# Moving one block of experts from place 7 to place 15 in the order of a mixture-of-experts stage

## The chip, the cores and the metric

The kernel runs on one core of one Trainium2 chip. The metric is the device time of one launch in microseconds (us). A profiled execution of the kernel before gave the trace that is read here. In the text PE is TensorE (matmul), DVE VectorE, ACT ScalarE, POOL GpSimd and SP SyncE; "L511" is line 511 of the kernel.

## The reference

One decoder block on 1024 tokens of width 1024, in float32: adaLN, a projection, gated linear attention and differential attention, a merge, and then a mixture of experts. Only the last part matters here:

```python
p_g = softmax(xf @ w_rg + b_rg);  p_top, g_idx = top_k(p_g, 1)
pe_top, e_loc = top_k(softmax(e_logits[group g_idx]), 2)       # two of the 8 experts of one group
weights = p_top * pe_top / sum(pe_top)
yb = (silu(xb @ w1[e]) * (xb @ w3[e])) @ w2[e]                 # w1, w3: 1024 x 512, w2: 512 x 1024
out[token] += yb * weight;      x = x + gate2 * out
```

There are 32 experts. Each has three matrices of 2 MB, so that all of them are 201 MB.

## The kernel before

The first 960 us or so are the attention part and the router. The expert stage follows and runs to the end.

**Blocks.** The experts are ranked by how many tokens chose them. A rank gets 2 to 4 groups of 32 rows (`PARTS`), and four groups make a block of 128 rows: 22 blocks in all. `TURN` (L51) is the order in which the blocks are worked, and `QUADS[n]` the four ranks of the block at place n. Some blocks hold one rank alone, as (4,4,4,4). Others hold two, as (26,26,27,27).

**Passes.** A block has three passes on PE. Pass 0 multiplies its rows by w1, pass 1 by w3 and pass 2 by w2. Each is 32 matmuls of a 32-column stationary tile against 512 columns (64 records in the trace, as float32 goes twice). From place 3 on, PE's order is: transposes of the hidden rows of block n-1 (L1431), passes 0 and 1 of block n, transposes of the rows of block n+1 (L1348), pass 2 of block n-1. This order stands in `PASSES` (L53).

**Weight buffers.** Ten buffers of 2 MB each hold one matrix. When a pass meets a matrix that isn't loaded yet, the planner (L63 to L69) gives it the buffer whose last use comes first, and `FREED_BY` notes the pass that frees it. SP walks the matrices in the order of their first use (L574 to L582). For each it waits until PE has done the freeing pass and then starts the load (L511). Ahead of its first matmul a pass waits for its matrices (L1410, L1441). The first 12 and the last 14 of these loads are cut in two halves (`HALVED`, L515 and L520), the 60 between them are whole. I number these 60 as F1 to F60. A block brings three loads for each rank in it that is new.

**POOL.** For each block POOL gathers the token rows (L722) and adds the results to the output by an indirect DMA with accumulation (L737). A block with two ranks has two such scatters, one behind the other.

Each matrix is loaded once. A rank whose groups lie in two blocks that stand far apart keeps its three buffers in between: rank 13 does so from place 4 to place 14, so that seven buffers turn over in that stretch.

The change reaches what depends on `TURN`: `QUADS`, `PASSES`, the planner's `BUF` and `FREED_BY`, the list of loads, the segments of the scatters and the column of the tables that a block reads.

Of the kernel before, what the change touches and what calls it, by code (L numbers as in the profile page):

```python
# [47 lines left out]
GROUPS = [r for r in range(NE) for _ in range(PARTS[r])]  # L48
NB = len(GROUPS) * G // P
assert NB * P == len(GROUPS) * G and NB % 2 == 0  # L50
TURN = (1, 0, 2, 16, 10, 17, 3, 19, 4, 7, 8, 9, 5, 18, 11, 12, 14, 13, 15, 20, 6, 21)  # L51
QUADS = [GROUPS[4 * v:4 * v + 4] for v in TURN]
PASSES = [(w, b) for b in range(3) for w in range(2)] + [(2, 0), (2, 1)] + [x for b in range(3, NB) for x in ((0, b), (1, b), (2, b - 1))] + [(2, NB - 1)]  # L53
NBUF = 10
# [15 lines left out]
LOADS = _n  # L70
assert len(set(QUADS[NB - 1])) == 2 and NB % 2 == 0 and TURN[NB - 1] >= NFB
LATE = list(FREED_BY)
# [49 lines left out]
def build(nc, io, out):  # L122

    with ExitStack() as ctx:
# [19 lines left out]
        def bank(b, n=1):  # L144
            return PS[:, b:b + n, :].rearrange("p b n -> p (b n)")
# [464 lines left out]
        def _(e):  # L610
# [107 lines left out]
            def gather(n, u):  # L718
                rows_done = NA * P if n == 0 else T
                if n >= 2:  # L720
                    e.wait_ge(s["m_tr"], 2 * n)
                e.indirect_dma_start(xg[u], None, xn_rows[0:rows_done],  # L722
                                     bass.IndirectOffsetOnAxis(tab_tok[:, TURN[n]:TURN[n] + 1], 0),
                                     bounds_check=rows_done - 1, oob_is_err=False).then_inc(xg_ld[u], 16)

            def scatter(n, u):
                e.wait_ge(s["m_y"], n + 2 if n < NB - 1 else n + 3)
                for i, (p0, p1) in enumerate(SEGS[n]):
                    if SEG_END[n] - len(SEGS[n]) + i > 0:
                        e.wait_ge(s["sc_done"], 16 * (SEG_END[n] - len(SEGS[n]) + i))  # L730
                    v = TURN[n]
                    idx = tab_tok[0:p1, v:v + 1] if p0 == 0 else seg_tok[0:p1 - p0, p0 // G - 1, v:v + 1]
# [1166 lines left out]
        def _(e):  # L1899
# [5 lines left out]
            def tsc(o, a, c1, op0, c2=None, op1=None):  # L1905
                if op1 is None:
                    return v.tensor_scalar(o, a, c1, None, op0)  # L1907
                return v.tensor_scalar(o, a, c1, c2, op0, op1)

            def stt(o, a, c, b, op0, op1):  # L1910
                return v.scalar_tensor_tensor(out=o, in0=a, scalar=c, in1=b, op0=op0, op1=op1)  # L1911
# [755 lines left out]
            def weighted(n, u):  # L2667
                e.wait_ge(s["m2_mm"], 2 * n + 3)
                if n >= 2:
                    e.wait_ge(s["sc_done"], 16 * SEG_END[n - 2])  # L2670
                stt(yb[u], bank(6, 2), tab_w[:, TURN[n]:TURN[n] + 1], gate[:, 1, :], ALU.mult, ALU.mult).then_inc(s["m_y"], 1)

# [16 lines left out]
            def same_rows():  # L2689
                e.wait_ge(s["mg_mm"], 1)  # L2690
                tsc(same, bank(5)[:, 0:P], tab_gap[:, TURN[NB - 1]:TURN[NB - 1] + 1], ALU.is_equal).then_inc(s["mg_in"], 1)
                e.wait_ge(s["mg_in"], 2)
# [59 lines left out]
```

## Time and profile before

| | us |
|---|---|
| median of 3 runs | 1499.81 (1498.01 to 1502.18) |
| the profiled execution's own time | 1502.34 |
| its span in the trace | 1500.6 |
| PE busy in the span | 1451.3 (97%) |
| PE's matmuls of all kinds | 8338 records |
| load queue of SP (q1) | 274.51 MB |
| POOL's DMA queue (q0) | 16.77 MB |

The span is the time from the first to the last instruction in the trace; the execution takes 1.7 us more. PE is busy nearly all the time, and the DMA engines are busy nearly all of the last third. The stage has to be read for both.

### The profile page before, as it was taken

Reading aid. Unit: us, or ns where it says so; the run is one execution under the profiler, and the core shown is the slowest. Engines: PE = TensorE matmul, PEld = TensorE weight load, DVE = VectorE, ACT = ScalarE, POOL = GpSimd, SP = SyncE. Lnnn points to the kernel's source line nnn. Section 1 sums busy time; section 2 is a strip of 40 time slices with the busy share of each in tenths; the row PEclk is TensorE's granted clock in tenths of the full one; section 3 lists DMA queues with packets and bytes.
Section 4 is the critical chain, followed back from the end, with each engine's and each line's share of the span. In section 5 each row is a group of like instructions: output and inputs, shape, how many; then the busy total and the mean of one; then the engine's idle time right before and its main releaser. Section 6 shows DMA issues by size and latency. Waiting matters only on the chain. (4 is left out here: it accounts for less than half of the span.)

```text
span 1500.6 us, 20824 instructions
## 1 busy us (share of the span) xinstructions
PE 1451.3 (97%) x8338; PEld 706.0 (47%) x8338; DVE 580.6 (39%) x1186; ACT 339.9 (23%) x674; POOL 109.4 (7%) x142
## 2 busy tenths in 40 slices
PE   7999999999999999999999999999998899999996
PEld 3444456887876555444444444543332233333332
DVE  4497444646474237322222455661111011111111
ACT  3513332333236333111111122311110011111110
POOL 2000000000000000000000001001111111111111
PEclk9999999999999999999999999999999999999999
DMA  9790100000012110211121842599999999999994
GB/s 355 256 354 1 64 1 1 29 29 29 29 57 57 29 28 1 56 42 42 42 98 49 327 155 111 210 349 403 417 406 418 401 366 378 405 416 405 405 413 163
DMA packets 80280, 292.48 MB, mean 195 GB/s; under 512 B 13408, under 2 KB 42302, under 8 KB 61505
## 3 DMA queue, kind: packets, MB, share of 16 engines
q1 hardware_dynamic: 73634, 274.51, 46.6%
q0 software_dynamic: 6560, 16.77, 4.4%
q8 instruction: 61, 1.00, 0.3%
q14 instruction: 25, 0.20, 0.0%
HBM read 277.47 MB, written 20.09 MB: 198 GB/s over the span
## 5 line engine op out<-in xcount | busy, mean ns | idle before, releaser
L779 PE MATMUL PS<-R 128*32 128x512 f32 (+6 forms) x3965 | 785.1, 566 | 22.7 <-DMA R<-in_ada_w 9.4
L779 PEld LDWEIGHTS PS<-R 128*32 128x32 f32 (+3 forms) x3965 | 291.4, 132 | 400.2 <-issue 372.2
L779 PE MATMUL PS<-HT,R 128*32 128x512 f32 (+2 forms) x1424 | 340.3, 599 | 3.8 <-DMA HT<-in_expert_w 2.2
L1903 DVE TENSOR_TENSOR R<-R,PS 128x512 f32<-128x512 f32 x131 | 95.6, 746 | 472.8 <-PE PS L779 472.8
L779 PE MATMUL PS<-R,HT 128*128 128x512 f32 (+1 forms) x672 | 235.4, 506 | 3.1 <-ACT R L1526 1.5
L779 PEld LDWEIGHTS PS<-HT,R 128*32 128x32 f32 (+1 forms) x1424 | 113.4, 128 | 149.0 <-issue 148.1
L779 PEld LDWEIGHTS PS<-R,HT 128*128 128x128 f32 x672 | 125.7, 191 | 94.2 <-issue 81.4
L1526 ACT ACTIVATE R<-PS 128x512 f32<-128x512 f32 (+4 forms) x119 | 71.3, 610 | 430.8 <-PE PS L779 295.6
L779 PE MATMUL PS<-WK,R 128*32 128x512 f32 (+1 forms) x464 | 107.9, 601 | 0.0
L1911 DVE SCALAR_TENSOR_TENSOR R<-PS,R,gate 128x1024 f32<-128x1024 f32 (+1 forms) x23 | 28.5, 1238 | 129.8 <-PE PS L779 123.3
L737 POOL DMA_INDIRECT out_rows<-R x36 | 52.3, 1453 | 303.0 <-DVE R L1911 160.6
L1526 ACT ACTIVATE R<-PS,att_nm 128x128 f32<-128x128 f32 (+7 forms) x64 | 46.8, 736 | 108.8 <-DVE att_nm L1907 108.8
L1526 ACT ACTIVATE R<-PS,S,A 128x128 f32<-128x128 f32 x92 | 34.4, 456 | 159.0 <-PE PS L1348 159.0
L1903 DVE TENSOR_TENSOR R<-R 128x512 f32<-128x512 f32 (+13 forms) x95 | 59.2, 638 | 19.1 <-PE PS L779 16.3
L1526 ACT ACT_TABLE_LOAD x30 | 38.5, 1283 | 96.1 <-PE PS L779 93.6
L1526 ACT ACTIVATE R<-R 128x512 f32<-128x512 f32 (+7 forms) x49 | 31.8, 655 | 104.3 <-DVE R L1903 100.3
L1526 ACT ACTIVATE WK<-R 128x128 f32<-128x128 f32 (+2 forms) x56 | 34.2, 611 | 80.5 <-DVE R L1903 77.4
L2122 DVE TENSOR_REDUCE att_mx<-PS 128x2 f32<-128x256 f32 (+7 forms) x32 | 43.3, 1354 | 20.6 <-PE PS L779 20.4
L1526 ACT ACTIVATE WK<-PS 128x512 f32<-128x512 f32 (+9 forms) x50 | 30.6, 611 | 87.3 <-PE PS L935 48.7
L1911 DVE SCALAR_TENSOR_TENSOR R<-R,cact 128x2048 f32<-128x2048 f32 (+1 forms) x23 | 46.6, 2026 | 3.0 <-DMA R<-in_ada_w 0.6
L779 PE MATMUL PS<-R,gate 128*128 128x256 f32 (+1 forms) x224 | 47.1, 366 | 0.0
L779 PE MATMUL PS<-R,WK 128*128 128x128 f32 (+1 forms) x352 | 44.6, 279 | 2.1 <-DVE R L1907 1.6
(263 smaller groups left out, 851.8 us busy)
## 6 DMA issues: line engine op xcount, KB each, us to landing
R<-in_expert_w SPq DMA_DIRECT2D x36, 2048.0 KB
R<-in_expert_w SPq DMA_DIRECT2D x46, 1024.0 KB, 15.6
HT<-in_expert_w SPq DMA_DIRECT2D x17, 2048.0 KB, 21.8
HT<-in_expert_w SPq DMA_DIRECT2D x18, 1024.0 KB, 12.5
R<-in_ada_w SPq DMA_DIRECT2D x16, 1024.0 KB, 7.0
WK<-in_expert_w SPq DMA_DIRECT2D x7, 2048.0 KB
R<-in_w_in SPq DMA_DIRECT2D x24, 512.0 KB, 3.9
R<-in_ada_w SPq DMA_DIRECT2D x16, 512.0 KB, 10.7
```

Of the source, the lines that this page charges most:

```text
L737: e.indirect_dma_start(out, bass.IndirectOffsetOnAxis(idx, 0), rows_out, None, compute_op=ALU.add, bounds_check=T - 1, oob_is_err=False).t ...
L779: return nc.tensor.matmul(o, l, r, start=a, stop=z)
L1526: return nc.scalar.activation(o, i, f, **kw)
L1903: return v.tensor_tensor(o, a, b, op)
L1911: return v.scalar_tensor_tensor(out=o, in0=a, scalar=c, in1=b, op0=op0, op1=op1)
L2122: att(v.tensor_reduce(att_mx[:, i % 2, :], score_v[:, :, 0:(i + 1) * P], AX.X, ALU.max))
```

## The change

The block of ranks 26 and 27 (block number 19) leaves place 7 and goes to place 15. The blocks of places 8 to 15 each move up by one place.

```diff
-TURN = (1, 0, 2, 16, 10, 17, 3, 19, 4, 7, 8, 9, 5, 18, 11, 12, 14, 13, 15, 20, 6, 21)
+TURN = (1, 0, 2, 16, 10, 17, 3, 4, 7, 8, 9, 5, 18, 11, 12, 19, 14, 13, 15, 20, 6, 21)
```

The ranks by place, with the number of new matrices that the block brings:

| place | 6 | 7 | 8 | 9 | 10 | 11 | 12 | 13 | 14 | 15 | 16 | 17 | 18 |
|---|---|---|---|---|---|---|---|---|---|---|---|---|---|
| before | 4 | 26,27 | 5 | 8,9 | 9,10 | 10,11 | 6 | 24,25 | 13,14 | 14,15 | 17,18 | 16 + 17 | 18,19 |
| new | 3 | 6 | 3 | 6 | 3 | 3 | 3 | 6 | 3 | 3 | 6 | 3 | 3 |
| after | 4 | 5 | 8,9 | 9,10 | 10,11 | 6 | 24,25 | 13,14 | 14,15 | 26,27 | 17,18 | 16 + 17 | 18,19 |
| new | 3 | 3 | 6 | 3 | 3 | 3 | 6 | 3 | 3 | 6 | 6 | 3 | 3 |

(Block 17 works rank 16 and a last group of rank 17.) Rank 13 now holds its buffers up to place 13. Places 0 to 6 and 16 to 21 hold the same blocks as before. The number of loads, their sizes and which of them are cut in two stay as they are. The sequence of loads is the same up to F10. From F11 on the matrices of ranks 26 and 27 stand later in it, and many matrices lie in another buffer with another freeing pass.

## Rows read from the trace of the kernel before

**Rows 1.** The page: span, DMA's busy tenths and GB/s in 40 slices.

```profile
span 1500.6 us, 20824 instructions
...
DMA  9790100000012110211121842599999999999994
GB/s 355 256 354 1 64 1 1 29 29 29 29 57 57 29 28 1 56 42 42 42 98 49 327 155 111 210 349 403 417 406 418 401 366 378 405 416 405 405 413 163
```

**Rows 2.** Stretches: length, busy us by engine, PE's clock, DMA share, GB/s.

```profile
1100.00:1200.00 100.00, 87.95 (x752) 29.34 (x748) 11.86 (x19) 9.28 (x20) 13.24 (x10) 0.95 1.01 409
1200.00:1260.00 60.00, 60.00 (x548) 19.77 (x544) 10.59 (x18) 7.49 (x17) 8.96 (x7) 1.00 0.97 366
1260.00:1400.00 140.00, 140.00 (x1280) 45.36 (x1276) 21.19 (x36) 16.77 (x37) 22.06 (x17) 1.00 1.01 407
1131.00:1135.50 4.50, 4.50 (x28) 1.47 (x31) 0.00 (x0) 0.00 (x0) 0.00 (x0) 0.62 1.02 391
1193.30:1197.50 4.20, 4.20 (x24) 1.38 (x28) 0.00 (x0) 0.00 (x0) 1.42 (x1) 0.59 1.02 437
```

**Rows 3.** PE by time: start, us, line, names, count, [idle before].

```profile
1119.28 7.07 PE L779 MATMUL PS<-R 128*32 128x512 f32 x64 [1.33 <-DMA R<-in_expert_w]
1126.28 0.66 PE L1431 MATMUL PS<-ident,R 128*128 128x128 f32 x4
1130.92 0.62 PE L779 MATMUL PS<-R 128*32 128x512 f32 x2 [3.98 <-DMA WK<-in_expert_w]
...
1141.90 8.77 PE L779 MATMUL PS<-HT,R 128*32 128x512 f32 x64 [2.21 <-DMA HT<-in_expert_w]
...
1159.22 13.94 PE L779 MATMUL PS<-R 128*32 128x512 f32 x128
...
1181.70 7.07 PE L779 MATMUL PS<-HT,R 128*32 128x512 f32 x64
1193.30 8.77 PE L779 MATMUL PS<-R 128*32 128x512 f32 x64 [4.53 <-DMA R<-in_expert_w]
```

**Rows 4.** Four loads at L511: ns, start us, us to landing.

```profile
L511 SPq DMA_DIRECT2D HT<-in_expert_w x1: 332/332/332, 1110.3 to 1110.3; - x1
...
DMA to landing us min/median/max: 31.5/31.5/31.5
...
L511 SPq DMA_DIRECT2D HT<-in_expert_w x1: 332/332/332, 1217.9 to 1217.9; - x1
...
DMA to landing us min/median/max: 15.5/15.5/15.5
...
L511 SPq DMA_DIRECT2D HT<-in_expert_w x1: 336/336/336, 1322.7 to 1322.7; - x1
...
DMA to landing us min/median/max: 21.5/21.5/21.5
...
L511 SPq DMA_DIRECT2D HT<-in_expert_w x1: 333/333/333, 1382.2 to 1382.2; - x1
...
DMA to landing us min/median/max: 24.2/24.2/24.2
```

**Rows 5.** SP by time, columns as in rows 3.

```profile
1232.79 0.33 SPq L511 DMA_DIRECT2D HT<-in_expert_w  x1
...
1240.38 0.33 SPq L511 DMA_DIRECT2D R<-in_expert_w  x1
```

**Rows 6.** PE and POOL at the end, columns as in rows 3.

```profile
1457.38 0.66 PE L1431 MATMUL PS<-ident,R 128*128 128x128 f32 x4
...
1465.83 0.62 PE L779 MATMUL PS<-HT,R 128*32 128x512 f32 x2 [0.79 <-DMA R<-in_expert_w]
...
1481.78 8.71 PE L779 MATMUL PS<-R 128*32 128x512 f32 x67 [0.87 <-ACT R L1526]
...
1492.43 1.56 POOL L737 DMA_INDIRECT out_rows<-R  x1 [8.41 <-DVE R L2706]
```

## The prediction

> **What bounds the kernel now.** I read the slices of the page first. DMA stands at 9 tenths or more in the last 14 slices, at some 400 GB/s, while PE stands at 97% over the whole span [rows 1]. So two engines are nearly full in the expert stage, and the busy shares don't say which one sets the end. The table of stretches goes further [rows 2]. From 1100 to 1200 us the DMA engines are full at 409 GB/s and PE stands still for 12.05 of 100 us. From 1200 to 1260 PE is busy for 60.00 of 60 us and DMA falls to 366 GB/s. From 1260 to 1400 both are full, PE with 140.00 of 140 us. PE's order of time shows where the 12 us are: 1.33 us ahead of pass 2 of block 5, 3.98 ahead of pass 0 of block 7 (ranks 26 and 27), 2.21 ahead of its pass 1, and 4.53 ahead of pass 1 of block 9 (ranks 8 and 9), each released by a weight load [rows 3]. These are the heavy blocks: six loads each against the three of others. At the end PE waits once more for a weight, 0.79 us ahead of pass 1 of block 21. From there it works with one short gap to the last scatter [rows 6].
>
> Two rates carry the rest. *PE:* a pass is 7.0 us, and a whole block 1181.70 - 1159.22 = 22.48 us [rows 3]. *Loads:* I number the whole loads F1 to F60. F14 is issued at 1110.3 and lands 31.5 us later, at 1141.8. F30 lands at 1217.9 + 15.5 = 1233.4, F49 at 1344.2 and F60 at 1406.4 [rows 4]. From F14 to F30 that is 91.6 / 16 = 5.72 us a load, from F49 to F60 62.2 / 11 = 5.65, and from F30 to F49 110.8 / 19 = 5.83. These 5.7 us hold POOL's gathers and scatters too, which share the engines. The middle stretch lost 19 x (5.83 - 5.70) = 2.5 us. That is where the queue ran short: F30 was issued only 15.5 us ahead of its landing, F32 at 1232.79 and F33 at 1240.38 [rows 5], 12.0 and 10.1 us ahead of the 1244.8 and 1250.5 that F14 and 5.72 us a load would give. A load can't be issued before PE has freed its buffer. Elsewhere a load waits 21 to 31 us in the queue [rows 4], and a later issue costs nothing.
>
> So the chain is the load queue. It runs without a break from before 1100 us to the landing that PE meets at 1465.8 [rows 6], but for the 2.5 us. PE's waits in the middle matter only if the last weights would come earlier without them.
>
> **The change, part by part.** *Work.* It removes no load, matmul, gather or scatter, and adds none. PE's 22 blocks stay at 22.48 us each. The gathers and scatters of POOL change places with their blocks, and those of the last six blocks are the same. SP passes as many waits as before. All this costs nothing while the load queue is full, since it only swaps equal pieces. *The queue's order.* Loads are the same up to F10, and F11 on are other matrices of the same size in the same queue, so F-k lands when it did, as long as SP can issue it in time. *PE's side* has to be worked through, with S(n) the start of pass 0 of block n.
>
> Block 7 is now rank 5 alone. F11, its first matrix, lands at 1130.9 - 5.7 = 1125.2, and PE is ready at 1126.28 + 0.6 = 1126.9 [rows 3]: the 3.98 us wait goes. S(8) = 1149.4 (ranks 8, 9), and F15 has landed at 1147.5. Its pass 1 comes at 1156.4 and needs F17, at 1141.8 + 3 x 5.72 = 1159.0: a wait of 2.6 us. Behind a wait PE's clock can fall: after the waits of 2.21 and 4.53 us the pass took 8.77 us instead of 7.07 [rows 3], and after those of 3.98 and 4.53 us the granted clock was 0.62 and 0.59 for some 4 us [rows 2], a mixture of the two levels 1.2 and 2.4 GHz. After 1.33 us of waiting the pass still took 7.07. I put 1.7 us on each wait over 2 us. Then S(9) = 1149.4 + 22.5 + 2.6 + 1.7 = 1176.2. Places 9 to 15 bring 27 loads, 154 us of the queue, for 157 us of PE, and PE meets no wait there: the closest is F44 (w3 of rank 27), which lands at 1344.2 - 5 x 5.72 = 1315.6, where PE comes at 1176.2 + 6 x 22.48 + 7.0 = 1318.1.
>
> *Does the queue run short?* The weakest place is again rank 6. F26 is freed by pass 2 of block 8, which ends at S(9) + 21.9, so it is issued at about 1198.4, and F27 at about 1206.0. By 5.72 us a load they land at 1210.4 and 1216.2, so the leads are 12.0 and 10.2 us. They were 12.0 and 10.1 before. I take the same loss of 2.5 us. There is a second thin place now, at F33 and F34 with leads of about 17 and 14.5 us. The nearest row is F30 with 15.5 us, where nothing was lost yet: 0.4 us. No reason excludes a smaller loss, so the bounds are -2.5 us (no shortage at all) and +6.3 us: if the second place costs as much as the first one did in GB/s, (409 - 366) / 409 x 60 us [rows 2].
>
> *The second half.* S(16) = 1176.2 + 7 x 22.48 = 1333.6, for ranks 17 and 18. Blocks 15 and 16 are now two heavy ones in a row. Pass 1 of block 16 comes at 1340.6 and needs F49, at 1344.2: a wait of 3.6 us, and 1.7 for the clock. Pass 2 of block 15 comes at 1353.9 and needs F51, at 1355.6: 1.7 us. S(17) = 1363.2, against 1368.0 before (1457.96 less 4 x 22.48, where 1457.38 + 0.6 is S(21) [rows 6]). S(21) = 1453.1, some 5 us ahead of before. But the first half of rank 31's w1 lands four half loads of 2.85 us ahead of 1465.7, at 1454.3, and that of its w3 at 1465.7 as before. So PE waits 1.2 us, works 7.0 us and waits again until 1465.8: about 3.3 us, where it was 0.79. What was gained in the middle is given back here, to the last microsecond.
>
> *The sum.* Landing that PE meets at 1465.8, by the order alone: 0. Queue shortage: +0.4. The clock after the new wait of 3.3 us at the end, which now stands on the chain: +1.7 (0 to 1.7). Together +2.1 us. On the profiled execution's 1502.34 us this is 1504.4 (span 1502.7). The median of the runs is 2.5 us lower than that execution, 1499.81, and on it the sum gives 1501.9 us, which is my number.
>
> **The rivals.** *A. PE sets the end, faster.* If the loads were no bound, the waits of 3.98, 2.21 and 4.53 us and their three slow passes (5.1 us) would go, and one wait of 2.6 us with 1.7 would come: S(21) = 1176.2 + 12 x 22.48 = 1446.0 instead of 1458.0, and the 0.79 us go as well. That is -12.8 us, 1487.0. It needs rank 31's w3 landed by 1453, 12.7 us ahead of what the queue does at 409 GB/s. Against it stands DMA's share of 1.01 with 407 GB/s from 1260 to 1400. The Trainium skill, DMA: Bandwidth & Descriptors, section "Anatomy of one DMA", gives 2.0 us plus the bytes at 436 GB/s, which for 2 MB is 4.8 us beside the fixed part. By that rate the 341 us from 1141.8 to 1483 would shrink by 21 us and this rival would hold. The trace does not agree: full engines moved 407 to 409 GB/s. A milder form is that the shortage alone goes: -2.5 us and at most -0.8 more, 1496.5.
>
> *B. The queue runs dry, slower.* Mechanism: from place 9 to 14 PE asks for 21 loads in 6 blocks, 135 us, and the queue could bring 23.6. So it catches up with PE, and each load can be issued only when a pass frees its buffer, with seven buffers in turn. Place: F24 to F34, issued from about 1190 to 1245. Price: one us at the end for each us that the load queue has nothing to do. It decides from the point where the lead of a load falls clearly under the 10 us of F33. If the two thin places cost 6.3 us instead of 2.9 and 3.4, that is +6.3 with the clock's 1.7: 1507.8. For it speaks that two light runs (places 9 to 11, 13 and 14) follow one another where before a heavy block stood ahead of them. Against it speaks that the leads I work out are equal to those of before.
>
> *C. The change moves no time.* The heavy block's waits turn up at blocks 15 and 16 instead, the clock doesn't fall at the end, and the time is 1499.8.
>
> **How the numbers follow.** About 0.3% (4.5 us) is what a measurement of this kernel can tell from no change: faster is below 1495.3, slower above 1504.3. The forecast (loads bind, 1499.9 to 1504.3) has 0.54. C has 0.06 and the mild form of A 0.06, within the same band. A in full has 0.10. B has 0.24. So faster 0.10, same 0.66, slower 0.24. The range reaches from the mild form of A, 1496.5, to B's 1507.8. It leaves out A in full and the far end of B.
>
> **What would show it.** Right: no wait at 1131, 1142 and 1193. New ones near 1159 (2.6 us, block 8), 1344 (3.6, block 16), 1355 and at 1462 to 1466 (3.3), each with a clock under 1.00 behind it where it is over 2 us. S(9) near 1176, S(21) near 1455. F49 and F60 landing at 1344 and 1406 within 1 us, and the pass after 1465.8 at 8.8 us. A shows as no PE wait after 1160 and S(21) near 1446. B shows as F49 landing at 1347 or later, with a stretch of 350 GB/s that is longer than 60 us. Wrong would be above all the step that F-k lands when it did: then the pace of the queue hangs on something that the order changes.

## The result, and the profile after

The changed kernel takes 1503.27 us (median of 17 runs, 1499.78 to 1505.80), the kernel before 1500.51 us (17 runs beside it). The ratio is 1.0017, with a 95% interval of 1.0011 to 1.0024: 2.6 us slower. A second comparison on another occasion gave 1.0025 (1.0014 to 1.0037). The profiled execution of the changed kernel took 1502.05 us.

Its page, with the rows that answer to those of [rows 1]:

```profile
span 1500.3 us, 20824 instructions
...
DMA  9780100000012110111121832699999999999993
GB/s 358 259 348 1 65 0 1 29 29 29 29 57 57 29 28 14 43 42 42 42 98 71 327 139 107 217 364 404 414 410 402 384 392 405 417 406 413 402 404 120
```

By the span the changed kernel is 0.3 us shorter, though its runs are slower. That is the first thing to set right. The attention part and the router run ahead of the change, and their length moves by some us from one execution to the next. I therefore measure from S(6), the start of pass 0 of block 6, where the two kernels still do the same. Here it is in the kernel before (start, duration, line, names, count):

```profile
1102.98 7.07 PE L779 MATMUL PS<-HT,R 128*32 128x512 f32 x64
```

and here PE of the changed kernel by time, with the waits in brackets, as in [rows 3]:

```profile
1100.22 7.07 PE L779 MATMUL PS<-HT,R 128*32 128x512 f32 x64
...
1115.12 7.07 PE L779 MATMUL PS<-R 128*32 128x512 f32 x64
...
1122.71 7.07 PE L779 MATMUL PS<-R 128*32 128x512 f32 x64
...
1156.33 8.77 PE L779 MATMUL PS<-R 128*32 128x512 f32 x64 [4.06 <-DMA R<-in_expert_w]
...
1341.30 1.07 PE L779 MATMUL PS<-WK,R 128*32 128x512 f32 x2 [3.18 <-DMA R<-in_expert_w]
...
1352.95 7.07 PE L779 MATMUL PS<-R 128*32 128x512 f32 x64 [1.94 <-DMA R<-in_expert_w]
```

S(6) is at 1102.98 before and at 1100.22 after. From there to the end of the span it is 397.6 us before and 400.1 us after. That is +2.5 us, near the 2.6 us of the runs. It is one pair of executions, and a second profile of the changed kernel (e9 below) gave +1.2. Times of before are shifted by -2.8 us from here on where they are set beside those of after.

The long waits at 1131, 1142 and 1193 of [rows 3] are gone. PE starts block 7 at 1122.71, with no wait. In their place stand 4.06 us ahead of pass 1 of block 8, 3.18 ahead of pass 1 of block 16 and 1.94 ahead of pass 2 of block 15. The stretches (columns as in [rows 2]) show that PE stands still for 4.06 us between 1100 and 1200, where it was 12.05, and for 5.12 between 1260 and 1400, where it was none:

```profile
1100.00:1200.00 100.00, 95.94 (x855) 31.26 (x857) 15.16 (x25) 11.38 (x25) 14.50 (x11) 0.98 1.00 397
1200.00:1260.00 60.00, 60.00 (x552) 19.65 (x548) 9.31 (x17) 7.49 (x17) 10.13 (x8) 1.00 1.01 399
1260.00:1400.00 140.00, 134.88 (x1212) 43.93 (x1207) 21.18 (x36) 16.18 (x36) 22.12 (x17) 0.99 1.01 409
1462.30:1466.50 4.20, 4.16 (x20) 1.15 (x24) 0.00 (x0) 0.00 (x0) 0.60 (x1) 0.50 0.90 338
```

The end, as in [rows 6]:

```profile
1450.78 0.66 PE L1431 MATMUL PS<-ident,R 128*128 128x128 f32 x4
...
1462.34 1.07 PE L779 MATMUL PS<-R 128*32 128x512 f32 x2 [3.91 <-DMA WK<-in_expert_w]
...
1480.81 9.14 PE L779 MATMUL PS<-R 128*32 128x512 f32 x68 [0.87 <-ACT R L1526]
...
1491.47 1.56 POOL L737 DMA_INDIRECT out_rows<-R  x1 [8.41 <-DVE R L2706]
```

S(21) is at 1450.78 + 0.6 = 1451.4, which is 351.2 us after S(6). It was 355.0 before. So PE comes to the last block 3.8 us earlier. But the first half of rank 31's w3 lands 362.1 us after S(6), against 362.9 before (taken at PE's next matmul, 0.1 us behind the landing), and PE now waits 3.91 us for it instead of 0.79. Behind this wait the granted clock is 0.50 for some 4 us (the last row of the stretches), the lower of the two levels. Pass 1 of block 21 ends only at 1471.9, 9.5 us instead of 7.0. The start of the last pass (1480.81) is 18.5 us behind the landing. It was 16.0 before (1481.78 - 1465.83). The difference of 2.5 us is the slow pass. The 2.5 us from S(6) to the end are made up of three pieces: the landing 0.7 us earlier (362.12 against 362.85), the slow pass +2.5, and +0.7 behind the start of the last pass. This last piece is the last scatter, which takes 8.8 us from its start (1491.47) to the end of the span, where it took 8.2 before (1492.43). In the 14 profiles that time lies between 8.0 and 8.8 us whatever the order, so it is not an effect of the change.

S(6) is a point of PE's, and the load queue stands differently to it in the two executions. F10 is the last load that both orders share. In the kernel before it landed at 1119.1, 16.2 us after S(6), and PE waited for it until 1119.28 [rows 3]. In the changed kernel it landed at 1086.1 + 28.7 = 1114.8, 14.6 us after S(6):

```profile
L511 SPq DMA_DIRECT2D R<-in_expert_w x1: 333/333/333, 1086.1 to 1086.1; - x1
...
DMA to landing us min/median/max: 28.7/28.7/28.7
```

Counted from F10's landing, the first half of rank 31's w3 lands 347.4 us later in the changed kernel and 346.5 us later before (1465.7 - 1119.1). So the landing that comes 0.7 us earlier from S(6) is 0.9 us later in the queue's own time. The last pass starts 366.0 us after F10 against 362.6: 3.4 us more, of which 2.5 are the clock. Whether the other 0.9 belong to the new order or to chance is taken up below.

### The profile page after: what moved, and what is told of

Its sections match the earlier page's. It is cut to its first block and busy times, and to the rows that moved or that the text cites. A ratio compares the mean times of both kernels' runs of the same rounds, so it can differ in the third digit from the quotient of the medians.

```text
span 1500.3 us, 20824 instructions
## 1 busy us (share of the span) xinstructions
PE 1451.1 (97%) x8338; PEld 704.8 (47%) x8338; DVE 580.6 (39%) x1186; ACT 340.3 (23%) x674; POOL 109.4 (7%) x142
## 5 line engine op out<-in xcount | busy, mean ns | idle before, releaser
L779 PE MATMUL PS<-R 128*32 128x512 f32 (+6 forms) x3965 | 807.7, 566 | 23.4 <-DMA R<-in_ada_w 10.1
L779 PEld LDWEIGHTS PS<-R 128*32 128x32 f32 (+3 forms) x3965 | 296.2, 132 | 384.7 <-issue 356.4
L779 PE MATMUL PS<-HT,R 128*32 128x512 f32 (+2 forms) x1392 | 324.7, 594 | 0.0
L779 PEld LDWEIGHTS PS<-HT,R 128*32 128x32 f32 (+1 forms) x1392 | 108.3, 128 | 152.7 <-issue 151.9
L779 PE MATMUL PS<-WK,R 128*32 128x512 f32 (+1 forms) x496 | 117.6, 611 | 3.6 <-DMA R<-in_expert_w 3.6
L779 PEld LDWEIGHTS PS<-WK,R 128*32 128x32 f32 (+1 forms) x496 | 34.0, 120 | 40.4 <-issue 40.4
## 6 DMA issues: line engine op xcount, KB each, us to landing
R<-in_expert_w SPq DMA_DIRECT2D x46, 1024.0 KB, 14.6
```

Source lines behind the costliest of these rows:

```text
L779: return nc.tensor.matmul(o, l, r, start=a, stop=z)
```

## The experiments

Each profile also has an end counted from its own S(6), as above. In 14 profiles S(6) itself lay between 1099.9 and 1103.3 us, with the same code ahead of it. That is why the column is steadier than the spans, and why a ratio needs many runs. The last column counts from F10's landing to the start of the last pass of PE. It is the steadier one where the queue binds, as S(6) is where PE binds. The landings of F10 and w3 are those of the trace.

| kernel | ratio to before (95% interval) | S(6) to w3 of rank 31 | S(6) to end | F10 to last pass |
|---|---|---|---|---|
| before | 1 | 362.9 | 397.6 | 362.6 |
| changed | 1.0017 (1.0011 to 1.0024) | 362.1 | 400.1 | 366.0 |
| changed, again (e9) | 1.0025 (1.0014 to 1.0037) | 362.5 | 398.8 | 365.1 |
| changed, clock kept up at the end (e1) | 1.0004 (0.9994 to 1.0013) | 361.1 | 396.2 | 362.3 |
| the same, again (e10) | 1.0011 (1.0000 to 1.0023) | 360.9 | 395.9 | 362.6 |
| before, clock kept up in the middle (e2) | 1.0006 (0.9996 to 1.0016) | 361.2 | 396.4 | 362.5 |
| before, light loads (e5) | 0.9996 (0.9985 to 1.0007) | 352.8 | 396.4 | 361.6 |
| changed, light loads (e6) | 0.9975 (0.9965 to 0.9986) | 349.1 | 394.0 | 359.9 |
| block at place 8 (e3) | 1.0005 (0.9996 to 1.0014) | 362.4 | 397.6 | 362.5 |
| block at place 10 (e4) | 1.0012 (1.0002 to 1.0022) | 365.5 | 403.5 | 367.9 |
| changed, places 19 and 20 exchanged (e7) | 1.0014 (1.0003 to 1.0025) | 355.4 | 397.3 | 363.0 |
| before, the same exchange (e8) | 0.9999 (0.9987 to 1.0011) | 355.1 | 396.4 | 361.3 |
| e8 with e2's edit (e11) | 1.0001 (0.9993 to 1.0010) | 354.9 | 395.3 | 361.1 |
| e7, clock kept up (e12) | 1.0004 (0.9995 to 1.0013) | 355.2 | 395.9 | 361.0 |

My theory was that the load queue sets when the last weights land, whatever PE gains in the middle, and that the loss is the slow clock behind the longer wait. The rivals were that the queue itself lost time, and that PE's own losses count.

**Keeping the clock up at the end.** PE does matmuls that nobody reads while it waits. The edit, in `up`:

```diff
+                        if k == 0:
+                            for _ in range({(21, 1): 16}.get((n, w), 0)):
+                                mm(bank(2 + w)[:, 0:P], ident[:, :], ident[:, :])
                         for r in sorted(set(q)):
```

> The changed order, with 16 matmuls that nobody reads (128x128 identity into the PSUM bank that pass 1 is about to overwrite) ahead of pass 1 of block 21, where PE waits 3.91 us in the changed kernel. Theory (the load queue sets when rank 31's w3 lands, and the whole loss against before is the slow clock behind that wait, where pass 1 took 9.5 us instead of 7.0): PE's clock stays up, the pass takes 7.0 us, and the time falls by about 2.5 us to that of the kernel before, ratio 1.000. Rival (the loss sits in the queue, which ran 1.7 us later from F14 to F60): the time stays at 1.0017 of before, and the pass still takes over 8.5 us or ends where it did.

PE at the end of this kernel:

```profile
1459.80 3.84 PE L779 MATMUL PS<-ident 128*128 128x128 f32 x32
...
1479.72 9.14 PE L779 MATMUL PS<-R 128*32 128x512 f32 x68 [0.87 <-ACT R L1529]
```

The 32 records at 1459.80 fill 3.84 us of the wait. The last pass starts 16.1 us behind the landing of w3 (1463.6, by the trace), as in the kernel before, not 18.5. From F10 to the start of the last pass it is 362.3 us, where the kernel before has 362.6 and the changed one 366.0. Of these 3.7 us the clock is 2.5. The rest is the landing of w3, 346.2 us after F10 and not 347.4. Up to 1459.80 the two kernels do the same, so this part varies between executions. The ratio fell from 1.0017 to 1.0004. I ran both once more side by side.

> The changed kernel again, word for word, beside the same with unread matmuls ahead of pass 1 of block 21. Theory (slow clock behind the last wait): 1.0015 to 1.0020 of before, with a wait of 3 to 4 us ahead of pass 1 of block 21 and a pass of 8.8 to 9.5 us behind it. A rival that the first figure was chance: 1.000.

> The changed kernel with the 16 unread matmuls ahead of pass 1 of block 21, again, on the same chip as the changed kernel itself. Theory: 1.0000 to 1.0005 of before, pass 1 of block 21 in 7.0 us, and from F14's landing to the start of the last pass 340 us as before, where the changed kernel has 343. Rival (the queue is what lost): the same ratio as the changed kernel and 342 us or more.

The changed kernel gave 1.0025 (6 runs) and the one with the matmuls 1.0011 (12 runs), both a little above what was expected. From F10 to the last pass the second has 362.6 us, as before. Twice the same edit brought 0.13 to 0.14% (2 us), in the direction and about the size of the theory. The intervals overlap in both pairs, so that the runs alone do not prove it; the traces carry the argument. From the landing of w3 to the start of the last pass it is 16.1 us in the kernel before, in e1, e2, e3 and e10, and 18.6 and 17.8 us in the two profiles of the changed kernel. What the runs do not settle is whether the queue, too, costs some tenths of a us: w3 landed 347.4 and 347.3 us after F10 in these two, and 346.2 and 346.5 in e1 and e10, which have the same order. In the second profile of the changed kernel the wait was 2.87 us:

```profile
1462.52 0.70 PE L779 MATMUL PS<-R 128*32 128x512 f32 x2 [2.87 <-DMA WK<-in_expert_w]
...
1480.17 9.14 PE L779 MATMUL PS<-R 128*32 128x512 f32 x68 [0.87 <-ACT R L1526]
```

From 1462.52 to the start of the last pass it is 17.7 us, 1.7 more than before. So the price of the slow clock differs by execution, 1.7 us here and 2.5 us there.

**Keeping the clock up in the middle of the kernel before.** The same edit with `{(7, 0): 16, (7, 1): 8, (9, 1): 18}`.

> The order of before, with matmuls that nobody reads in its three long waits: 16 ahead of pass 0 of block 7, 8 ahead of its pass 1, 18 ahead of pass 1 of block 9. They keep PE's clock up, so that the three passes take 7.0 us each and PE reaches block 21 some 5 us earlier. Theory (the load queue binds to the end): no gain. PE waits longer ahead of block 21 instead, 0.8 us becomes 4 to 5, and if the clock falls behind it the kernel is even slower than before by about 2 us: ratio 1.000 to 1.002. Rival (PE's own lost time in the middle counts): 4 to 5 us faster, ratio 0.997.

```profile
1122.26 3.74 PE L779 MATMUL PS<-ident 128*128 128x128 f32 x32
1126.36 0.62 PE L779 MATMUL PS<-R 128*32 128x512 f32 x2 [0.37 <-DMA WK<-in_expert_w]
...
1137.35 7.07 PE L779 MATMUL PS<-HT,R 128*32 128x512 f32 x64 [1.93 <-DMA HT<-in_expert_w]
...
1177.51 7.07 PE L779 MATMUL PS<-HT,R 128*32 128x512 f32 x64 [1.99 <-DMA HT<-in_expert_w]
1184.51 4.29 PE L779 MATMUL PS<-ident 128*128 128x128 f32 x36
...
1461.10 0.62 PE L779 MATMUL PS<-HT,R 128*32 128x512 f32 x2 [2.31 <-DMA R<-in_expert_w]
...
1477.05 9.14 PE L779 MATMUL PS<-R 128*32 128x512 f32 x68 [0.87 <-ACT R L1529]
```

Pass 1 of block 7 took 7.07 us instead of 8.77, and PE reached block 21 351.9 us after S(6) (1461.10 - 2.31 - 7.0, less 1099.9) instead of 355.0. It then waited 2.31 us at the end instead of 0.79, and the time was the same, 1.0006. From F10 to the last pass it is 362.5 us against 362.6. The wait was shorter than the 4 to 5 us expected, and no slow pass followed it. What PE wins in the middle, this kernel doesn't keep. A gain of 0.3% is excluded.

**Light loads.** Here w1 and w3 of ranks 16 and 19, late in the queue, are loaded to a quarter. These experts are worked with stale weights, and 6 MB are left out of the queue.

```diff
-                    e.dma_start((ew_down if w == 2 else ew_up)[j], (w1_v, w3_v, w2_v)[w][ex]).then_inc(ew_ld[j], 16)
+                    n = 2 if w < 2 and r in (16, 19) else 4 if w == 2 else 8
+                    e.dma_start((ew_down if w == 2 else ew_up)[j][:, 0:n, :],
+                                (w1_v, w3_v, w2_v)[w][ex][:, 0:n, :]).then_inc(ew_ld[j], 16)
```

> The order of before, but of four matrices late in the queue (w1 and w3 of ranks 16 and 19, needed by blocks 17 and 18) only a quarter is loaded, 1.5 MB of each left out, so that the experts of these ranks are worked with stale weights. That takes 4 x 0.75 x 5.7 = 17 us out of the queue behind F49. Theory (at the end PE and the queue are in balance, since PE has lost 16 us in its three middle waits and has not waited after them): only the 0.79 us wait ahead of block 21 goes, ratio 0.999 to 1.000, and S(21) lies where it was. Rival (the queue alone binds the kernel before): 4 us or more faster, ratio 0.997 or less.

> The changed order with the same four matrices loaded to a quarter. Theory (the changed order does free PE in the middle, and the queue takes the gain back at the end): the 3.91 us wait ahead of pass 1 of block 21 goes with its slow pass of 2.5 us, while those of block 8 and 16 stay, since their loads come before the lightened ones. The kernel is then 6.4 us faster than the changed one, some 3.5 us faster than before (ratio 0.9975), and faster than the order of before with the same light loads. Rival (the change frees nothing, the heavy block costs PE as much at place 15): ratio to before as the order of before with light loads.

In the order of before, the last blocks' transposes and the last pass:

```profile
1456.36 0.66 PE L1433 MATMUL PS<-ident,R 128*128 128x128 f32 x4
...
1479.77 9.14 PE L781 MATMUL PS<-R 128*32 128x512 f32 x68 [0.87 <-ACT R L1528]
```

and in the changed order, from block 8 on:

```profile
1156.79 9.66 PE L781 MATMUL PS<-R 128*32 128x512 f32 x64 [4.22 <-DMA R<-in_expert_w]
...
1341.48 0.62 PE L781 MATMUL PS<-WK,R 128*32 128x512 f32 x2 [2.01 <-DMA R<-in_expert_w]
...
1353.15 8.77 PE L781 MATMUL PS<-R 128*32 128x512 f32 x64 [3.57 <-DMA R<-in_expert_w]
...
1451.79 0.66 PE L1433 MATMUL PS<-ident,R 128*128 128x128 f32 x4
...
1475.20 9.14 PE L781 MATMUL PS<-R 128*32 128x512 f32 x68 [0.87 <-ACT R L1528]
```

Both figures came out as the theory gave them: 0.9996 and 0.9975. In neither is there a wait for a load after 1400 us, and the landing of w3 is 10 and 13 us earlier than in the same order with full loads. The order of before has nothing to gain from it, since PE still reaches block 21 355.0 us after S(6). The changed order reaches it after 352.1 us, pays no wait, and is 0.2% faster than the other, with intervals that overlap by 0.0001. This is the clearest result of the study. The change does free PE in the middle, and only the queue at the end takes the gain back.

**Other places for the block.** Only `TURN` is changed: `(1, 0, 2, 16, 10, 17, 3, 4, 19, 7, 8, 9, ...)` and `(1, 0, 2, 16, 10, 17, 3, 4, 7, 8, 19, 9, ...)`.

> The block of ranks 26 and 27 at place 8, one place later than before. Blocks 8 and 9 are then two heavy ones in a row, and the light run 9, 10, 11 of the changed kernel comes two blocks later. Theory (queue shortage in a light run, one us at the end for one us without work in the queue): the heavy pair puts PE behind the queue, F26 and F27 are no longer short, the 2.5 us of shortage go and the last loads land about 3 us earlier than in the kernel before. PE waits ahead of block 8 pass 1 (2.8) and block 9 pass 1 (3.7). At the end there is a wait of some 2 us with its slow pass, so the gain is 1 to 3 us: ratio 0.998 to 0.999. Rival (place of the heavy block doesn't matter to the queue): landings as before, ratio 1.000 to 1.002.

> The same block at place 10. The queue then meets a light run (places 9 and 7), six loads for the heavy block and a second light run with buffers freed late. By the leads worked out for each load there are two shortages, 3.3 us at F26 and F27 and 3.2 us at F29. Theory: the last loads land about 3 us later than before, and with the slow pass at the end the kernel is 5 us slower, ratio 1.003 to 1.004. Rival (shortages don't add up, the queue catches up): ratio 1.000 to 1.002, last landing within 1 us of before relative to the start of the stage.

The block at place 8:

```profile
1158.72 8.45 PE L779 MATMUL PS<-R 128*32 128x512 f32 x64 [4.21 <-DMA R<-in_expert_w]
...
1186.83 1.07 PE L779 MATMUL PS<-HT,R 128*32 128x512 f32 x3 [4.04 <-DMA R<-in_expert_w]
...
1463.80 0.62 PE L779 MATMUL PS<-HT,R 128*32 128x512 f32 x2 [3.85 <-DMA R<-in_expert_w]
...
1479.75 9.14 PE L779 MATMUL PS<-R 128*32 128x512 f32 x68 [0.86 <-ACT R L1526]
```

```profile
1463.80:1468.00 4.20, 4.20 (x40) 1.56 (x44) 0.00 (x0) 0.00 (x0) 0.55 (x1) 1.00 0.89 325
```

The waits in the middle stand where I put them (4.21 and 4.04 us, for 2.8 and 3.7). No load from F20 to F32 had a lead under 14.5 us, so the queue never ran short. And yet the last weights landed no earlier: 362.4 us from S(6), against 362.9, and 346.4 us from F10, against 346.5. The gain of 1 to 3 us did not come. My reading that the short stretch of before costs 2.5 us falls with it. The second fence shows something else. After a wait of 3.85 us the granted clock stayed at 1.00, where after 3.91 us in the changed kernel it was 0.50.

The block at place 10, first one load of the light run, then the stretch around it, then PE:

```profile
L511 SPq DMA_DIRECT2D HT<-in_expert_w x1: 332/332/332, 1221.4 to 1221.4; - x1
...
DMA to landing us min/median/max: 8.2/8.2/8.2
```

```profile
1200.00:1225.00 25.00, 18.51 (x152) 5.96 (x148) 2.25 (x5) 2.10 (x5) 3.85 (x3) 0.86 0.83 305
```

```profile
1212.03 1.07 PE L779 MATMUL PS<-R 128*32 128x512 f32 x2 [6.49 <-DMA HT<-in_expert_w]
...
1466.88 1.07 PE L779 MATMUL PS<-HT,R 128*32 128x512 f32 x2 [3.51 <-DMA R<-in_expert_w]
...
1485.51 4.93 PE L779 MATMUL PS<-R 128*32 128x512 f32 x44 [0.87 <-ACT R L1526]
```

Here F29 was issued only 8.2 us ahead of its landing, and from 1200 to 1225 the engines moved 305 GB/s. This shortage reached the end: w3 of rank 31 landed 365.5 us from S(6), 2.6 later than before. With the slow clock at the end (1485.51 - 1466.88 = 18.6 us) this execution was 5.9 us longer than before. The runs say less: 1.0012, at most 1.0022, so that the expected 1.003 is excluded. The profiled execution, with 1506.65 us, was the slowest of this kernel's runs, and its 6.49 us wait is not to be taken for the usual one.

**Exchanging places 19 and 20.** `TURN` ends in `15, 6, 20, 21` instead of `15, 20, 6, 21`.

> The changed order, and in addition the blocks of places 19 and 20 exchanged: rank 7 alone at 19, ranks 28 and 29 at 20. Of the loads that follow rank 31's w3 in the queue there are then four instead of three, so that this matrix lands one load, 5.7 us, earlier. Theory (the wait ahead of pass 1 of block 21 is where the queue binds): that wait goes, the clock stays up, and a smaller wait (2 us) comes ahead of pass 2 of block 20. 2 to 3 us faster than the changed kernel and about as much as 0 to 1.5 us faster than before: ratio 0.999 to 1.000. Rival (the total of the queue's bytes sets the end whatever the order): ratio 1.0017 as the changed kernel.

> The order of before with the same exchange of places 19 and 20. Theory (PE's middle waits bind as much as the queue): only the 0.79 us wait can go, ratio 0.9995 to 1.000, no PE wait for a load after 1200 us. Rival (the queue alone binds): 2 to 4 us faster, ratio 0.998.

The changed order with the exchange, and the order of before with it:

```profile
1468.29 0.81 PE L779 MATMUL PS<-WK,R 128*32 128x512 f32 x2 [3.70 <-DMA R<-in_expert_w]
...
1478.50 9.14 PE L779 MATMUL PS<-R 128*32 128x512 f32 x68 [0.86 <-ACT R L1526]
```

```profile
1477.32 9.14 PE L779 MATMUL PS<-R 128*32 128x512 f32 x68 [0.87 <-ACT R L1526]
```

The first half of w3 landed one load earlier, 355 us after S(6). With the changed order the wait for w3 went. A wait of 3.70 us ahead of pass 2 of block 20 came in its place, larger than the 2 us expected and with a granted clock of 0.57 behind it, and the runs show no gain, 1.0014: the queue binds there just as well. With the order of before there is no wait for a load after 1200 us, as expected, and no gain either, 0.9999. The queue alone does not bind that kernel.

The exchange also has a price of its own at the end. Place 20 now holds a block of two ranks, with two scatters one behind the other. PE's last pass starts 1.3 us earlier from F10 than before (361.3 against 362.6), but the last scatter waits for these two:

```profile
1483.40 1.41 POOL L737 DMA_INDIRECT out_rows<-R  x1 [3.96 <-DMA out_rows<-R]
1488.60 1.57 POOL L737 DMA_INDIRECT out_rows<-R  x1 [3.79 <-issue]
```

It starts 11.3 us behind the last pass (1488.60 - 1477.32), where it was 10.65 before [rows 6]. In e7, e11 and e12 it is 11.2 to 11.3 too. So 0.6 us of what the exchange could bring are lost in POOL, and these four runs say less about the queue than the light loads do.

**Both at once.**

> The order of before with the blocks of places 19 and 20 exchanged, and the unread matmuls in the three middle waits. The exchange takes the queue's bound at the end away by one load, the matmuls give PE back the slow clock of the middle. Theory (PE and queue bind alike, so that only both together gain): 1 to 3 us faster than before, ratio 0.998 to 0.9995, faster than either edit alone, and a first small wait at the end. Rival: 1.000 as each alone.

> The changed order with the same exchange, and unread matmuls ahead of pass 1 of block 8 and 16 and pass 2 of blocks 15 and 20, where it waits. Theory: the queue's last landing binds, and without a slow pass behind the wait of block 20 the time is that of the same order of loads with PE free: 1 to 2 us faster than before, ratio 0.9985 to 0.9995. Rival (the exchange brings nothing with the changed order, as its first figure of 1.0014 says): 1.001 or more.

```profile
1470.55 0.62 PE L779 MATMUL PS<-R 128*32 128x512 f32 x2 [1.16 <-DMA HT<-in_expert_w]
...
1479.06 9.14 PE L779 MATMUL PS<-R 128*32 128x512 f32 x68 [0.86 <-ACT R L1529]
```

```profile
1465.47 3.74 PE L779 MATMUL PS<-ident 128*128 128x128 f32 x32
...
1477.79 9.14 PE L779 MATMUL PS<-R 128*32 128x512 f32 x68 [0.86 <-ACT R L1531]
```

From S(6) these two profiles are 2.3 and 1.7 us shorter than before. From F10 they reach the last pass 1.5 and 1.6 us earlier, and POOL takes 0.6 of it back. Their runs show no gain: 1.0001 and 1.0004, where at most 0.9995 was expected of both. No version here beats the kernel before by what can be measured.

## Why the prediction was right

The forecast was 1501.9 us, or +2.1 us on the median. The kernel moved by +2.6 us, in the range, and by the mechanism that the forecast named: the queue sets when w3 lands, and the loss is the slow clock behind the new wait. That the sum came within 0.5 us is in part luck, since its terms were off in both directions. Point by point, with the times of the prediction shifted by -2.8 us:

- *F-k lands when it did.* F17 was put at 1156.2 and PE met it at 1156.33. F49: 1341.4, met at 1341.30. F51: 1352.8, met at 1352.95. Rank 31's w3: 1462.9, met at 1462.34. This step carried the whole, and at these four it held within 0.6 us. (In the thin stretch F26 landed some 2.5 us later from S(6) than in the kernel before, which did not reach the end.)
- *The waits.* Block 8: 2.6 expected, 4.06 measured. The prediction took S(7) from the kernel before, where PE had still waited 1.33 us ahead of it [rows 3]. In this execution pass 2 of block 5 began at 1115.12 without a wait. Block 16: 3.6, measured 3.18. Block 15: 1.7, measured 1.94. At the end 3.3, measured 3.91. The 3.3 is a slip: by the prediction's own numbers PE starts at 1454.3, works 7.0 us and waits from 1461.3 to 1465.8, which is 4.5 us. The small wait ahead of pass 0 of block 21 did not come, as PE was 1.1 us later there than worked out. It was ready for pass 1 when expected, and the 3.91 us are 0.6 less than 4.5 because w3 landed 0.6 us earlier than put.
- *The middle gain.* PE was to be 4.9 us ahead at S(21) and was 3.8 ahead. It was all given back, as said.
- *The clock.* The place was right and the size was not. I took 1.7 us from the passes of 8.77 us, and the pass took 9.5 us, so 2.5. In the second profile it was 1.7. The terms of the sum were 0 for the order, +0.4 for the shortage and +1.7 for the clock. From S(6) the profiles show -0.7 at the landing of w3, +2.5 for the clock and +0.7 in the last scatter, a piece that the sum did not have and that varies by as much between executions. The sentence that a wait over 2 us brings the slow clock and one of 1.33 doesn't is too simple (below).
- *The queue's shortage.* The leads were nearly right:

```profile
1195.81 0.33 SPq L511 DMA_DIRECT2D HT<-in_expert_w  x1
...
1203.40 0.33 SPq L511 DMA_DIRECT2D R<-in_expert_w  x1
```

  F26 and F27 were issued 13.7 and 10.5 us ahead of their landing (I had put 12.0 and 10.2). In the kernel before they were 14.4 and about 12 by the completions of F32 and F33 in the trace (1247.2 and 1252.3), not the 12.0 and 10.1 that I worked out. The size of the loss can't be read from S(6), where the last weights land 0.7 us earlier. From F10 they land 0.9 us later, but the same order shows 0.3 us earlier in e1 and 0.0 in e10. So the +0.4 is neither confirmed nor refuted. And place 8, with no thin place, did not bring back the 2.5 us that I read as lost in the kernel before. There the fall to 366 GB/s [rows 2] was not time lost at the end. Why the average between two landings was larger there was not settled. The 2.5 us of lost time that the prediction took over from it were not lost.
- *Rival A* (PE sets the end, 1487) fell by the trace, and e5 and e6 show under which condition it would hold: 6 MB less in the queue, and then only 3.7 us (0.9975) and not 12.8, since the waits of blocks 8, 16 and 15 stay. The estimate from the 436 GB/s of the Trainium skill (DMA: Bandwidth & Descriptors, section "Anatomy of one DMA") finds no support here: full engines moved 397 to 409 GB/s. The page fits that figure to transfers that GpSimd issues, and SyncE issues these loads.
- *Rival B* (the queue runs dry) did not happen in the changed order. Place 10 shows the mechanism: 2.6 us later at the last weights, once a lead had fallen to 8.2 us. In the changed kernel, with 10.5 us, it was 0.9 us at most, so it decides somewhere near these leads.
- *Rival C* (no time moved) is excluded by both ratios. The clock at the end did fall. With it kept up (e1, e10) the time is nearly C's.
- A reading of [rows 1] was off and changes nothing: DMA stands at 9 tenths in 13 slices, and the last one is at 4.

## What to carry to other kernels

Where a full transfer queue and a full engine run side by side, moving a heavy block moved the engine's waits and hardly the end (places 8, 10 and 15): first count what the queue still has to deliver behind the last wait. Before counting the removed waits as a gain, take a few late loads away in both orders. It shows at once which order has slack, and how much of it the queue holds back. And compare from a point ahead of the change that both traces share, since the part before it can differ by more than the effect. Take this point on the side that binds. Here a load's landing (F10) gave the same 362.3 to 362.6 us in five profiles, while the same five lay 1.8 us apart from S(6).

## What the hardware showed that I had not expected

Whether PE's clock falls behind a wait is not settled by the wait's length alone in these traces. After 3.91 us (changed kernel), 3.51 us (place 10) and 2.87 us (e9) it fell. After 3.85 us (place 8) it stayed at 1.00. After 2.02 us in e1 (block 16) the next pass took 8.7 us, after 2.03 us in e8 (block 7) it took 7.07. The slow clock cost 1.7 us in one execution of the changed kernel and 2.5 us in another. What decides it was not tested.

A load queue with only two loads waiting need not lose time at the end. In the kernel before, leads fell to about 12 us and the stretch to 366 GB/s, and w3 landed 346.5 us after F10. At place 8, where no lead was under 14 us and the stretch from 1200 to 1260 moved 397 GB/s, it was 346.4.
